# Loading the per-layer-embedding inputs later and storing their product from the ScalarE queue

## The chip, the cores and the metric

The kernel runs on one core of one Trainium2 chip. Five engines work side by side and meet at semaphores: TensorE (PE, its weight loads as PEld), VectorE (DVE), ScalarE (ACT), GpSimd (POOL) and SyncE (SP). The metric is the device time of one launch in microseconds. Transfers are issued from the instruction streams of SP, ACT and POOL and are carried out by 16 DMA engines that all of them share.

## The reference

Two transformer blocks over 512 tokens of width 1024, all in float32. The first has an mLSTM and differential attention mixer and then a mixture of experts; the second has pooling and window attention, a feed-forward layer and, at its very end, a gate over a product of per-layer inputs (`p_2`, 256 wide). The parts that matter here:

```python
def hierarchical_moe(h, ...):                      # first block, 32 experts, top 2 of one group
    g_sel = argmax(h @ w_group + b_group);  top_vals, top_idx = top_k(expert logits of the group, 2)
    ... sort the 1024 (token, expert) pairs by expert ...
    hid = silu(xb @ w_gate[e]) * (xb @ w_up[e]);  y = hid @ w_down[e]
    ...
def second_block(x, p, ..., w_ple, w_ple_gate, b_ple_gate):
    ...
    gate = sigmoid(h @ w_ple_gate + b_ple_gate)
    h = h + gate * (p @ w_ple)                     # p: 512 x 256, w_ple: 256 x 1024
```

`p @ w_ple` depends on nothing but inputs, so it can be computed at any time before the last line.

## The kernel before

The program is a hand-ordered instruction list for each engine. Work meets through counting semaphores; the eight PSUM banks are shared by "turns": `open_turn` waits until the bank's last reader has left it, `fill_turn` marks it full, `filled` waits for that, and `leave` and `left` mark and await that it is empty again. Which instruction stands where is only what is written in each engine's function.

The change lies in the passage from the mixer to the experts, about 335 to 395 us. What happens there:

- The last output projection pieces (`out_piece`), the residual, the second norm (`HN`), and its transposes (`turn_h`) give `HT`; `route(t)` multiplies it by the router weights. The normed rows are also stored to `h_rows` by ACT (`store_rows`), from where the experts' tokens are gathered.
- DVE turns the logits into one-hot choices (to `oh_ready`), PE counts ranks ("rank"), DVE makes positions (to `slots_hot`), PE multiplies them out ("slots"), DVE writes the indices, and POOL gathers the first block of token rows (L1140).
- PE transposes those rows (`turn_rows(0)`, L676), ACT copies them rounded into `XTS` (`rows_hi(0)`, L1423), DVE subtracts to get the rest (`rows_lo(0)`, L1945), and only then can the first expert product run (L687). Weights are split the same way: ACT writes a rounded copy `HI` in seven parts (`weights_hi`, L1419), DVE the remainder (`weights_lo`, L1940).
- The two small inputs of the last line are used here as well: `PIN` (p, 0.5 MB) and `PLEW` (w_ple, 1 MB) are loaded by two DMAs on the ACT queue (L1377, L1378), PE transposes PIN (four turns "pt"), ACT copies the transposes to `PET` (L1398), PE makes the product in eight pieces (`extra(n)`, L644), ACT copies each out of PSUM into one of three buffers (`extra_out(n)`, L1407), and SP stores it to `ple_rows` in HBM (L1016). Just before the end of the program it is read back.

The `extra` pieces stand on PE between the routing steps as filler: four before "rank", two before "slots", two behind. ACT interleaves its eight `extra_out` with the seven weight parts of expert 0. SP loads the experts' weights, three loads of 2 MB for each expert; the first load of the expert loop waits for `gate_raw_used`, which PE signals when the first product of the first expert block is done. 32 expert blocks follow one another in a loop.

Of the kernel before, what the change touches and what calls it, by code (L numbers as in the profile page):

```python
# [23 lines left out]
ACT = mybir.ActivationFunctionType  # L24
AX = mybir.AxisListType.X

P = 128
T = 512
D = 1024
TT = T // P  # L30
# [67 lines left out]
def build(nc, A, out):  # L98
    ctx = ExitStack()

    def sb(name, shape, dt=F32):
        return ctx.enter_context(nc.sbuf_tensor(name, shape, dt))

    def sem(name):
        return ctx.enter_context(nc.semaphore(name))

    with ctx:
# [4 lines left out]
        HT = sb("HT", [P, DT, T])  # L112
# [35 lines left out]
        def m(a, *shape):  # L148
            v = M[:, a:a + int(np.prod(shape))]
            if len(shape) == 2:  # L150
                v = v.rearrange("p (a b) -> p a b", a=shape[0])
            if len(shape) == 3:
                v = v.rearrange("p (a b c) -> p a b c", a=shape[0], b=shape[1])
            return v
# [36 lines left out]
        P2, DM = m(9936, TT), m(9940, TT)  # L191
# [28 lines left out]
        H5S = [as_r(f"h5s{k}", M_AT + a, DT, T) for k, a in enumerate((0, 8192))]  # L220
        GT = m(4096, 2, 512)
        OUT2 = m(12288, 2, TT, 512)
        PLEW, PIN, PET, PLE3 = m(12928, 2, D), m(1024, TT, 2 * P), m(16896, 2, T), m(2560, 3, 512)

        ps = ctx.enter_context(nc.psum_tensor("ps", [P, 8, 512], F32))
        h_rows = nc.dram_tensor("h_rows", [T, D], F32, kind="Internal").ap()
        ple_rows = nc.dram_tensor("ple_rows", [T, D], F32, kind="Internal").ap()
# [35 lines left out]
        r_dve = sem("r_dve")  # L263
        r_act = sem("r_act")
# [53 lines left out]
        ple_in = sem("ple_in")  # L318
        ple_out = [sem(f"ple_out{k}") for k in range(3)]
# [9 lines left out]
        def open_turn(pe, key, bank):  # L329
            turn[key] = (bank, turns_of[bank])  # L330
            if turns_of[bank]:
                pe.wait_ge(empty[bank], turns_of[bank])
            turns_of[bank] += 1
            return ps[:, bank, :]

        def fill_turn(ins, key):
            ins.then_inc(full[turn[key][0]], 1)

        def filled(eng, key):
            eng.wait_ge(full[turn[key][0]], turn[key][1] + 1)  # L340
            return ps[:, turn[key][0], :]

        def leave(ins, key):
            ins.then_inc(empty[turn[key][0]], 1)

        def left(eng, key):
            eng.wait_ge(empty[turn[key][0]], turn[key][1] + 1)
# [70 lines left out]
        def _(pe):  # L418
            def transposes(key, bank, src, n, width=P, idn=None):

                o = open_turn(pe, key, bank)
                idn = ident[:, :] if idn is None else idn
                for c in range(n):
                    ins = pe.transpose(o[:, c * width:(c + 1) * width], src[:, c * P:(c + 1) * P], idn)  # L424
                fill_turn(ins, key)
# [182 lines left out]
            def turn_h(t):  # L608
                for c in range(2):
                    pe.wait_ge(hn_ready, t + 1 + (c if t == TT - 1 else 0))  # L610
                    transposes(("h2", t, c), 2 + (2 * t + c) % 4, HN[:, t, c * 512:(c + 1) * 512], 4)

            def route(t):
                left(pe, ("h2", t, 0))
                left(pe, ("h2", t, 1))
                for k in range(DT):
                    ins = pe.matmul(ps[:, 7, t * E:(t + 1) * E], HT[:, k, t * P:(t + 1) * P], WR[:, k, :],
                                    start=(k == 0), stop=(k == DT - 1))
                return ins
# [11 lines left out]
            turn_h(2)  # L631
            out_piece(1, 3, 0, DT, 1)
            route(2)
            pe.wait_ge(ple_in, 32)
            for t in range(TT):
                transposes(("pt", t), t, PIN[:, t, :], 2)
            turn_h(3)
            fill_turn(route(3), "route")

            def extra(n):  # L640
                c, t = divmod(n, TT)
                o = open_turn(pe, ("pl", n), n % 4)
                for k in range(2):
                    ins = pe.matmul(o, PET[:, k, t * P:(t + 1) * P], PLEW[:, k, c * 512:(c + 1) * 512],  # L644
                                    start=(k == 0), stop=(k == 1))
                fill_turn(ins, ("pl", n))

            for t in range(TT):
                left(pe, ("pt", t))
            for n in range(4):  # L650
                extra(n)

            pe.wait_ge(oh_ready, 1)
# [3 lines left out]
                    ins = pe.matmul(o[:, t * NE:(t + 1) * NE], UPPER if j == t else ONESB,  # L657
                                    OHS[:, j, :], start=(j == 0), stop=(j == min(t, TT - 1)))
            fill_turn(ins, "rank")
            for n in range(4, 6):  # L660
                extra(n)

            pe.wait_ge(slots_hot, 1)
# [1 line left out]
            for j in range(2 * TT):  # L665
                ins = pe.matmul(o[0:BLK, 0:BLOCKS_HELD], POS1H[:, j, :], BLKV[:, j, :], start=(j == 0), stop=(j == 2 * TT - 1))
            fill_turn(ins, "slots")
            for n in range(6, 8):
                extra(n)


# [184 lines left out]
            for j, u in enumerate(FF_UNITS):  # L856
                n = int(u[-1])
# [47 lines left out]
            for c in range(2):  # L905
# [4 lines left out]
                for t in range(TT):  # L910
                    n = c * TT + t
# [16 lines left out]
        def _(sp):  # L928
# [80 lines left out]
            for s, u in last_use.items():  # L1009
                used_up(sp, u)  # L1010
                dst, src = first_loads[s]
                sp.dma_start(dst, src).then_inc(slot_in[s], 16)
            for n in range(2 * TT):
                c, t = divmod(n, TT)
                left(sp, ("pl", n))
                sp.dma_start(ple_rows[t * P:(t + 1) * P, c * 512:(c + 1) * 512], PLE3[:, n % 3, :]).then_inc(ple_out[n % 3], 16)  # L1016
            sp.wait_ge(tab_ready, 1)

            def freed(e, k):
# [24 lines left out]
            for n in range(2 * TT):  # L1044
                c, t = divmod(n, TT)
# [159 lines left out]
        def _(act):  # L1205
# [119 lines left out]
            def final_out(i, kind):  # L1325
                dst, gain = (MIXA, R_AN) if kind == "d" else (HT, R_MN)
                key = ("F", i, kind)
                q = filled(act, key).rearrange("p (h t) -> p h t", h=HEADS)
                leave(act.activation(dst[:, 0:HEADS, i * P:(i + 1) * P], q, ACT.Copy, scale=prm[:, gain:gain + 1]), key)
# [44 lines left out]
                        act.wait_ge(x_kept, t + 1)  # L1374
                        square_x(t)
            final_out(TT - 1, "m")
            act.dma_start(PIN, A["p_2"][0, 0].rearrange("(t p) c -> p t c", p=P)).then_inc(ple_in, 16)  # L1377
            act.dma_start(PLEW, A["w_ple_2"][0].rearrange("(k p) c -> p k c", p=P)).then_inc(ple_in, 16)  # L1378

            def store_rows(u):  # L1380
                act.wait_ge(hn_ready, u + 1 if u < TT - 1 else TT + 1)
                act.dma_start(h_rows[u * P:(u + 1) * P, :], HN[:, u, :]).then_inc(h_out, 16)
# [7 lines left out]
            for c in range(2):  # L1390
                left(act, ("o", c, TT - 1))
                acc = (7, 82)[c]
                act.activation(JUNK3[:, c * 512:(c + 1) * 512], X[:, TT - 1, c * 512:(c + 1) * 512], ACT.Square,
                               accum_out=st[:, acc:acc + 1]).then_inc(sumsq, 1)
                if c == 0:
                    store_rows(2)
            for t in range(TT):
                leave(act.activation(PET[:, :, t * P:(t + 1) * P],  # L1398
                                     filled(act, ("pt", t))[:, 0:2 * P].rearrange("p (k t) -> p k t", k=2), ACT.Copy), ("pt", t))
            leave(act.activation(HT[:, 4:8, (TT - 1) * P:T],  # L1400
                                 filled(act, ("h2", TT - 1, 1)).rearrange("p (k t) -> p k t", k=4), ACT.Copy), ("h2", TT - 1, 1))
            store_rows(3)

            def extra_out(n):
                if n >= 3:
                    act.wait_ge(ple_out[n % 3], 16 * (n // 3))
                leave(act.activation(PLE3[:, n % 3, :], filled(act, ("pl", n)), ACT.Copy), ("pl", n))  # L1407

            act.wait_ge(r_dve, 1)
            act.activation(EXPG, D4, ACT.Exp).then_inc(r_act, 1)  # L1410


            def weights_hi(e, part, odd):

                u, a, b = PARTS[part]
                s, c = expert_slots(odd)[u], slice(a, b)
                if a == 0:
                    act.wait_ge(slot_in[s], raw_loads(e, odd, s))
                act.activation(HI[u][:, c], ring[:, s, c], ACT.Copy).then_inc(w_hi, 1)  # L1419
# [38 lines left out]
            for part in range(7):  # L1458
                if part == 5:
                    filled(act, "slots")  # L1460
                    act.wait_ge(wts_ready, 1)
                weights_hi(0, part, 0)
                extra_out(part)
                if part == 2:
                    act.wait_ge(r_dve, 2)
                    act.activation(P2, DM, ACT.Exp).then_inc(r_act, 1)
            extra_out(7)
            act.wait_ge(tab_ready, 1)
            rows_hi(0)
            act.preload_act_table(ACT.Silu)  # L1470
# [671 lines left out]
```

## Time and profile before

| | us |
|---|---|
| median of 3 runs | 1514.16 (1513.98 to 1516.74) |
| the profiled execution | 1516.74 |
| its span in the trace | 1515.0 |
| PE busy | 1430.0 (94%) |
| DVE busy | 930.9 (61%) |
| ACT busy | 752.2 (50%) |

The profiled execution is the slowest of the three. Times in a trace count from the start of its span. "Released by" or "<-" names what ended a wait. A time inside the passage is read from the timeline of one engine: start, duration, line, operation, and how long the engine had idled before. float32 matmuls appear as two passes, so that one `extra` piece (two matmuls in the program) is four passes in the trace.

### The profile page before, as it was taken

What the parts mean: (1) busy time and instruction counts of PE and PEld (TensorE: products, weight loads), DVE (VectorE), ACT (ScalarE), POOL (GpSimd) and SP (SyncE); (2) the same over time, 40 slices, a digit from 0 to 9 for tenths busy, and PEclk for the clock granted to TensorE, in tenths of its full rate; (3) what the DMA queues carried; (4) which work ended last, traced back from release to release, by engine and by line L of the source; (5) the groups of instructions that cost most, each with busy time, mean ns of one, the idle gap of its engine ahead of it and who ended that gap; (6) DMA issues with size and microseconds to landing.
All of it is one profiled execution on the core that took longest, in us unless ns stands there. A gap on an engine that the chain in (4) does not pass through costs nothing.

```text
span 1515.0 us, 19584 instructions
## 1 busy us (share of the span) xinstructions
PE 1430.0 (94%) x6529; PEld 1047.6 (69%) x6530; DVE 930.9 (61%) x1129; ACT 752.2 (50%) x930; POOL 200.6 (13%) x234
## 2 busy tenths in 40 slices
PE   6899999999899999999999977988989999999998
PEld 6787667555677777777777754544468888888886
DVE  6845453354899999998989954272544413442275
ACT  4334334123699999998989840242124310333031
POOL 1011001000222222222212210041100000000010
PEclk8999999999999999999999997998989999999999
DMA  6131104315699999999999978300003321333231
GB/s 224 56 111 57 56 29 170 154 30 213 259 404 407 412 410 416 409 417 406 404 411 413 394 229 262 111 1 29 0 1 112 111 96 71 111 111 129 80 111 56
DMA packets 67892, 298.56 MB, mean 197 GB/s; under 512 B 18110, under 2 KB 20220, under 8 KB 55548
## 3 DMA queue, kind: packets, MB, share of 16 engines
q1 hardware_dynamic: 55036, 273.76, 46.6%
q10 hardware_dynamic: 7440, 15.63, 2.9%
q0 software_dynamic: 5360, 8.40, 1.7%
q8 instruction: 37, 0.61, 0.2%
q14 instruction: 19, 0.16, 0.0%
HBM read 292.00 MB, written 14.94 MB: 203 GB/s over the span
## 4 chain that ended last, share of the span: by engine, by line
PE 73%; DMA 6%; DVE 5%; issue 2%; ACT 2%; POOL 0%; ACTq 0%; DVEq 0%; SPq 0%; POOLq 0%
PE ps L687 12%; PE ps L869 12%; PE ps L887 11%; PE ps L725 6%; DMA ring<-in_w_gate 5%; PE ps L543 4%; PE ps L846 4%; PE ps L718 4%; PE ps L922 3%; PE ps L696 3%; PE ps L473 2%; PE ps L747 2%; PE ps L424 2%; PE ps L771 1%; PE ps L676 1%
## 5 line engine op out<-in xcount | busy, mean ns | idle before, releaser
L1940 DVE TENSOR_TENSOR ring_r<-ring,hi 128x2048 fp32r<-128x2048 f32 (+1 forms) x224 | 431.2, 1982 | 19.1 <-ACT hi L1419 17.1
L1419 ACT ACTIVATE hi<-ring 128x2048 fp32r<-128x2048 f32 (+1 forms) x224 | 363.0, 1662 | 13.3 <-DMA ring<-in_w_gate 8.3
L887 PE MATMUL ps<-ring_r,ats 128*128 128x512 f32 x768 | 174.7, 389 | 0.0
L887 PEld LDWEIGHTS ps<-ring_r,ats 128*128 128x128 f32 x768 | 144.1, 188 | 29.9
L1605 DVE TENSOR_TENSOR ring_r<-ring,ring_r 128x4096 fp32r<-128x4096 f32 x18 | 79.7, 4425 | 131.5 <-ACT ring_r L1225 131.5
L1225 ACT ACTIVATE ring_r<-ring 128x4096 fp32r<-128x4096 f32 x18 | 65.2, 3624 | 150.7 <-PE ps L887 122.0
L1088 POOL TENSOR_TENSOR rsv<-msv,half 128x1 f32<-128x1 f32 (+2 forms) x32 | 39.1, 1222 | 751.3 <-DVE msv L1565 731.4
L687 PE MATMUL ps<-ring_r,XTS 128*128 128x512 f32 x512 | 128.5, 393 | 3.9 <-DVE XTS L1945 2.1
L687 PE MATMUL ps<-hi,XTS 128*128 128x512 f32 x512 | 126.4, 389 | 0.0
L869 PE MATMUL ps<-ring_r,ring_r 128*128 128x512 f32 x512 | 123.3, 394 | 1.8 <-DVE hi L2056 1.8
L473 PE MATMUL ps<-ring_r,ring_r 128*128 128x512 f32 x448 | 117.2, 411 | 7.6 <-DVE M L1636 4.5
L725 PE MATMUL ps<-hi,HIDS 128*64 128x512 f32 x512 | 123.6, 394 | 0.0
L687 PEld LDWEIGHTS ps<-ring_r,XTS 128*128 128x128 f32 x512 | 96.9, 190 | 27.1 <-issue 4.9
L869 PEld LDWEIGHTS ps<-ring_r,ring_r 128*128 128x128 f32 x512 | 97.5, 191 | 22.6 <-issue 2.2
L687 PEld LDWEIGHTS ps<-hi,XTS 128*128 128x128 f32 x512 | 96.1, 188 | 20.0
L725 PEld LDWEIGHTS ps<-hi,HIDS 128*64 128x64 f32 x512 | 69.2, 135 | 50.0 <-issue 1.6
L473 PEld LDWEIGHTS ps<-ring_r,ring_r 128*128 128x128 f32 x448 | 85.4, 196 | 25.4 <-DVE M L1636 4.9
L718 PE MATMUL ps<-ring_r,HIDS 128*64 128x512 f32 x256 | 67.4, 407 | 6.2 <-ACT HIDS L1443 4.1
L696 PEld LDWEIGHTS ps<-M 128*128 128x128 f32 x512 | 64.5, 191 | 7.5 <-issue 3.6
L696 PE MATMUL ps<-M 128*128 128x64 f32 x512 | 64.8, 272 | 3.1 <-ACT M L1428 3.1
L1146 POOL DMA_INDIRECT results<-M,idx x33 | 49.1, 1488 | 128.8 <-ACT M L1451 128.4
L869 PE MATMUL ps<-hi,ring_r 128*128 128x512 f32 x256 | 63.2, 389 | 0.0
(307 smaller groups left out, 1851.7 us busy)
## 6 DMA issues: line engine op xcount, KB each, us to landing
ring<-in_w_up SPq DMA_DIRECT2D x32, 2048.0 KB, 18.4
ring<-in_w_gate SPq DMA_DIRECT2D x32, 2048.0 KB
ring<-in_w_down SPq DMA_DIRECT2D x32, 2048.0 KB, 16.9
ring<-in_w_ff SPq DMA_DIRECT2D x16, 2048.0 KB, 8.4
ring<-in_w_in SPq DMA_DIRECT2D x8, 2048.0 KB, 8.5
ring<-in_w_out SPq DMA_DIRECT2D x2, 2048.0 KB, 8.6
M<-results ACTq DMA_DIRECT2D x8, 512.0 KB, 7.5
ring<-in_w_ple_gate SPq DMA_DIRECT2D x2, 2048.0 KB, 7.8
```

The lines of the kernel that those rows point to most:

```text
L473: ins = pe.matmul(o, a, b, start=(i == 0 and k == 0), stop=(i == 2 and k == DT - 1))
L543: ins = pe.matmul(ps[:, bank, :], a, w[:, k, :], start=(k == 0), stop=(k == DT - 1))
L687: ins = pe.matmul(ps[:, u, :], XTS[:, k, :, :].rearrange("p s b -> p (s b)"), w[:, k, :], start=(part == 1 and k == 0), stop=(part == 0 an ...
L696: ins = pe.matmul(ps[:, bank, f * BLK:(f + 1) * BLK], GUS[:, u, f * P:(f + 1) * P], SUM2[:, 0:BLK], start=True, stop=True)
L718: ins = pe.matmul(ps[0:BLK, 4 + c, :], HIDS[:, 0, f, :], w_rest[:, f, c * 512:(c + 1) * 512], start=(f == 0), stop=False)
L725: ins = pe.matmul(ps[0:BLK, 4 + c, :], HIDS[:, a, f, :], w_top[:, f, c * 512:(c + 1) * 512], start=False, stop=(a == 1 and f == FT - 1))
L869: ins = pe.matmul(o, w[a][:, k, f * P:(f + 1) * P], HTS[b][:, k, :], start=(i == 0 and k == 0), stop=(i == 2 and k == DT - 1))
L887: ins = pe.matmul(ps[:, 2 * t + c, :], ATS[a][:, 4 * (n % 4) + k, t * P:(t + 1) * P], w[b][:, k, c * 512:(c + 1) * 512], start=(n % 4 == 0 ...
L1225: act.activation(split_hi[j % 2][:, :], ring[:, s, :], ACT.Copy).then_inc(s_hi, 1)
L1419: act.activation(HI[u][:, c], ring[:, s, c], ACT.Copy).then_inc(w_hi, 1)
L1605: vec.tensor_tensor(ring_r[s][:, :], ring[:, s, :], split_hi[j % 2][:, :].bitcast(F32), ALU.subtract).then_inc(s_lo, 1)
L1940: vec.tensor_tensor(ring_r[s][:, c], ring[:, s, c], HI[u][:, c].bitcast(F32), ALU.subtract).then_inc(w_lo, 1)
```

## The change

On SP the eight stores to `ple_rows` are gone; ACT issues each of them, right behind the copy that fills the buffer, once that copy has ended. On ACT the loads of PLEW and PIN move from before the square of row tile 2 to behind the square of the last half tile, and PLEW now goes first; the four PET copies move behind the last `HT` copy and the last `store_rows`; two `extra_out` and both small exponentials (EXPG, P2) now stand ahead of the first weight part, the other six `extra_out` behind parts 0, 1, 2, 4, 5 and 6. On PE the transposes of PIN move behind the last `route`, and use banks 4 and 5 in turn instead of banks 0 to 3; the pieces are dealt 2, 3, 3 instead of 4, 2, 2. PIN lies 512 elements further in `M`.

```diff
-        ... PIN ... m(1024, TT, 2 * P)
+        ... PIN ... m(1536, TT, 2 * P)
@@ tensor
             route(2)
-            pe.wait_ge(ple_in, 32)
-            for t in range(TT):
-                transposes(("pt", t), t, PIN[:, t, :], 2)
             turn_h(3)
             fill_turn(route(3), "route")
...
+            pe.wait_ge(ple_in, 32)
+            for t in range(TT):
+                transposes(("pt", t), 4 + t % 2, PIN[:, t, :], 2)
             for t in range(TT):
                 left(pe, ("pt", t))
-            for n in range(4):
+            for n in range(2):
                 extra(n)
... rank ...
-            for n in range(4, 6):
+            for n in range(2, 5):
                 extra(n)
... slots ...
-            for n in range(6, 8):
+            for n in range(5, 8):
                 extra(n)
@@ sync
-            for n in range(2 * TT):
-                c, t = divmod(n, TT)
-                left(sp, ("pl", n))
-                sp.dma_start(ple_rows[...], PLE3[:, n % 3, :]).then_inc(ple_out[n % 3], 16)
             sp.wait_ge(tab_ready, 1)
@@ scalar
             final_out(TT - 1, "m")
-            act.dma_start(PIN, ...).then_inc(ple_in, 16)
-            act.dma_start(PLEW, ...).then_inc(ple_in, 16)
...
-            for t in range(TT):
-                leave(act.activation(PET[...], filled(act, ("pt", t)) ...), ("pt", t))
+            act.dma_start(PLEW, ...).then_inc(ple_in, 16)
+            act.dma_start(PIN, ...).then_inc(ple_in, 16)
             leave(act.activation(HT[:, 4:8, (TT - 1) * P:T], ...), ("h2", TT - 1, 1))
             store_rows(3)
+            for t in range(TT):
+                leave(act.activation(PET[...], filled(act, ("pt", t)) ...), ("pt", t))
 
             def extra_out(n):
+                c, t = divmod(n, TT)
                 if n >= 3:
                     act.wait_ge(ple_out[n % 3], 16 * (n // 3))
                 leave(act.activation(PLE3[:, n % 3, :], filled(act, ("pl", n)), ACT.Copy), ("pl", n))
-
+                left(act, ("pl", n))
+                act.dma_start(ple_rows[...], PLE3[:, n % 3, :]).then_inc(ple_out[n % 3], 16)
+
+            extra_out(0)
+            extra_out(1)
             act.wait_ge(r_dve, 1)
             act.activation(EXPG, D4, ACT.Exp).then_inc(r_act, 1)
+            act.wait_ge(r_dve, 2)
+            act.activation(P2, DM, ACT.Exp).then_inc(r_act, 1)
...
                 weights_hi(0, part, 0)
-                extra_out(part)
-                if part == 2:
-                    act.wait_ge(r_dve, 2)
-                    act.activation(P2, DM, ACT.Exp).then_inc(r_act, 1)
-            extra_out(7)
+                if part in (0, 1, 2, 4, 5, 6):
+                    extra_out((2, 3, 4, None, 5, 6, 7)[part])
```

On PE, between the router products (L617) and the transposes of the first gathered rows (L676), a piece of the difference of the two orders; L424 are transposes, L644 (L641 in the changed file) the `extra` pieces, L657 "rank", L666 "slots":

```order
 L617 MATMUL ps<-M,HT 128x36 x8
-L424 MATMUL ps<-ident,M 128x128 x16
+L424 MATMUL ps<-ident,M 128x128 x8
 L617 MATMUL ps<-M,HT 128x36 x8
-L644 MATMUL ps<-M 128x512 x8
+L424 MATMUL ps<-ident,M 128x128 x8
+L641 MATMUL ps<-M 128x512 x4
 L657 MATMUL ps<-M 128x32 x14
-L644 MATMUL ps<-M 128x512 x4
+L641 MATMUL ps<-M 128x512 x6
 L666 MATMUL ps<-M 64x58 x8
-L644 MATMUL ps<-M 128x512 x4
+L641 MATMUL ps<-M 128x512 x6
```

The eight transposes of PIN have moved behind the last router product, two pieces (four matmuls) stand ahead of "rank" instead of four, and three instead of two on each side of "slots".

On ACT, before, from the loads of PIN and PLEW (L1377, L1378) to the first small exponential (L1410); L1334 and L1393 are squares, L1382 stores of `h_rows`, L1398 the PET copies, L1400 the last `HT` copy:

```order
L1377 DMA M<-in_p 128x4x256
L1378 DMA M<-in_w_ple 128x2x1024
L1334 ACTIVATE M,st<-X 128x1024
L1382 DMA h_rows<-M 128x1024 x2
L1393 ACTIVATE M,st<-X 128x512
L1382 DMA h_rows<-M 128x1024
L1393 ACTIVATE M,st<-X 128x512
L1398 ACTIVATE M<-ps 128x2x128 x4
L1400 ACTIVATE HT<-ps 128x4x128
L1382 DMA h_rows<-M 128x1024
L1410 ACTIVATE M<-M 128x16
```

The same place afterwards, from the square of row tile 2 (L1330 now) to the first copy of a piece (L1403), with the squares at L1386, the stores of `h_rows` at L1375 and the PET copies at L1396:

```order
L1330 ACTIVATE M,st<-X 128x1024
L1375 DMA h_rows<-M 128x1024 x2
L1386 ACTIVATE M,st<-X 128x512
L1375 DMA h_rows<-M 128x1024
L1386 ACTIVATE M,st<-X 128x512
L1390 DMA M<-in_w_ple 128x2x1024
L1391 DMA M<-in_p 128x4x256
L1392 ACTIVATE HT<-ps 128x4x128
L1375 DMA h_rows<-M 128x1024
L1396 ACTIVATE M<-ps 128x2x128 x4
L1403 ACTIVATE M<-ps 128x512
```

Both loads now stand behind the last square, and the last store of `h_rows` stands behind them in the same queue.

On ACT again, the weight parts of expert 0 (copies into `hi`), before, with the copies of the pieces at L1407 and the exponential P2 at L1466:

```order
L1410 ACTIVATE M<-M 128x16
L1419 ACTIVATE hi_57<-ring 128x2048
L1407 ACTIVATE M<-ps 128x512
L1419 ACTIVATE hi_57<-ring 128x1024
L1407 ACTIVATE M<-ps 128x512
```

And afterwards, with the copies at L1403 and their stores at L1405:

```order
L1403 ACTIVATE M<-ps 128x512
L1405 DMA ple_rows<-M 128x512
L1403 ACTIVATE M<-ps 128x512
L1405 DMA ple_rows<-M 128x512
L1410 ACTIVATE M<-M 128x16
L1412 ACTIVATE M<-M 128x4
L1421 ACTIVATE hi_57<-ring 128x2048
L1403 ACTIVATE M<-ps 128x512
L1405 DMA ple_rows<-M 128x512
L1421 ACTIVATE hi_57<-ring 128x1024
```

The first weight part now stands behind two copies and their stores, and each later copy has a DMA issue between it and the next weight part.

## Rows read from the trace of the kernel before

**Rows 1.** The page, chain of waits by engine, whole span.
```profile
PE 73%; DMA 6%; DVE 5%; issue 2%; ACT 2%; POOL 0%; ACTq 0%; DVEq 0%; SPq 0%; POOLq 0%
```

**Rows 2.** Chain of waits in time, expert loop: start us, us, what.
```profile
674.11 19.57 DMA ring<-in_w_gate
```

**Rows 3.** The same view, 325 to 425 us.
```profile
364.38 8.64 PE ps L644 x16
...
378.91 1.15 PE ps L666 x16
...
383.06 4.56 DVE ring_r L1940 x3
...
387.64 0.70 DVE XTS L1945
...
389.05 8.94 PE ps L687 x32
```

**Rows 4.** Timeline of ACT: start us, us, engine, line, operation, idle before.
```profile
335.77 0.39 ACTq L1377 DMA_DIRECT2D M<-in_p  x1
336.19 0.53 ACTq L1378 DMA_DIRECT2D M<-in_w_ple  x1
336.84 1.06 ACT L1334 ACTIVATE M<-X 128x1024 f32<-128x1024 f32 x1 [0.39 <-issue]
...
358.12 0.63 ACT L1393 ACTIVATE M<-X 128x512 f32<-128x512 f32 x1 [12.16 <-DVE X L1777]
...
367.14 1.91 ACT L1419 ACTIVATE hi<-ring 128x2048 fp32r<-128x2048 f32 x1 [1.68 <-DMA h_rows<-M]
368.96 0.58 ACT L1407 ACTIVATE M<-ps 128x512 f32<-128x512 f32 x1
369.44 1.05 ACT L1419 ACTIVATE hi<-ring 128x1024 fp32r<-128x1024 f32 x1
370.38 0.59 ACT L1407 ACTIVATE M<-ps 128x512 f32<-128x512 f32 x1
...
372.28 0.21 ACT L1466 ACTIVATE M<-M 128x4 f32<-128x4 f32 x1
...
387.01 0.60 ACT L1423 ACTIVATE XTS<-ps 128x512 fp32r<-128x512 f32 x1 [1.76 <-PE ps L676]
```

**Rows 5.** Timeline of PE.
```profile
358.83 1.07 PE L424 MATMUL ps<-ident,M 128*128 128x128 f32 x8
...
379.98 3.70 PE L644 MATMUL ps<-M 128*128 128x512 f32 x8
386.23 0.68 PE L676 MATMUL ps<-ident,M 64*128 64x64 f32 x8 [2.55 <-DMA M<-h_rows,idx]
```

**Rows 6.** Timeline of PE's weight loads, two consecutive passes of the pieces.
```profile
365.49 0.34 PEld L644 LDWEIGHTS ps<-M 128*128 128x128 f32 x1 [0.51 <-issue]
366.35 0.34 PEld L644 LDWEIGHTS ps<-M 128*128 128x128 f32 x1 [0.52 <-issue]
```

**Rows 7.** Timeline of SP.
```profile
357.32 0.33 SPq L1012 DMA_DIRECT2D ring<-in_w_up  x1
369.56 16.03 SPq L1016 DMA_DIRECT2D ple_rows<-M  x8
392.73 0.36 SPq L1028 DMA_DIRECT2D ring<-in_w_gate  x1
```

**Rows 8.** DMA issues, 325 to 400 us: count, KB each, us from issue to landing.
```profile
M<-in_w_ple ACTq DMA_DIRECT2D x1, 1024.0 KB, 7.4
M<-in_p ACTq DMA_DIRECT2D x1, 512.0 KB, 3.5
```

**Rows 9.** The same view, 355 to 392 us.
```profile
ring<-in_w_up SPq DMA_DIRECT2D x1, 2048.0 KB, 8.5
ple_rows<-M SPq DMA_DIRECT2D x8, 256.0 KB, 2.0
h_rows<-M ACTq DMA_DIRECT2D x1, 512.0 KB, 5.4
```

**Rows 10.** Windows: busy of each engine, then PE clock, DMA share, GB/s.
```profile
360.00:365.00 5.00, 3.65 (x26) 3.19 (x27) 2.05 (x5) 1.09 (x3) 0.00 (x0) 0.98 0.98 409
365.00:366.00 1.00, 1.00 (x2) 0.34 (x1) 0.83 (x6) 0.22 (x1) 0.00 (x0) 0.50 0.26 102
```

More of the change, by code:

```diff
@@ L222, in build @@
         OUT2 = m(12288, 2, TT, 512)
-        PLEW, PIN, PET, PLE3 = m(12928, 2, D), m(1024, TT, 2 * P), m(16896, 2, T), m(2560, 3, 512)
+        PLEW, PIN, PET, PLE3 = m(12928, 2, D), m(1536, TT, 2 * P), m(16896, 2, T), m(2560, 3, 512)
         ps = ctx.enter_context(nc.psum_tensor("ps", [P, 8, 512], F32))
@@ L1012, in _ @@
                 sp.dma_start(dst, src).then_inc(slot_in[s], 16)
-            for n in range(2 * TT):
-                c, t = divmod(n, TT)
-                left(sp, ("pl", n))
-                sp.dma_start(ple_rows[t * P:(t + 1) * P, c * 512:(c + 1) * 512], PLE3[:, n % 3, :]).then_inc(ple_out[n % 3], 16)
             sp.wait_ge(tab_ready, 1)
@@ L1376, in _ @@
             final_out(TT - 1, "m")
-            act.dma_start(PIN, A["p_2"][0, 0].rearrange("(t p) c -> p t c", p=P)).then_inc(ple_in, 16)
-            act.dma_start(PLEW, A["w_ple_2"][0].rearrange("(k p) c -> p k c", p=P)).then_inc(ple_in, 16)
             def store_rows(u):
@@ L1396, in _ @@
                     store_rows(2)
+            act.dma_start(PLEW, A["w_ple_2"][0].rearrange("(k p) c -> p k c", p=P)).then_inc(ple_in, 16)
+            act.dma_start(PIN, A["p_2"][0, 0].rearrange("(t p) c -> p t c", p=P)).then_inc(ple_in, 16)
+            leave(act.activation(HT[:, 4:8, (TT - 1) * P:T],
+                                 filled(act, ("h2", TT - 1, 1)).rearrange("p (k t) -> p k t", k=4), ACT.Copy), ("h2", TT - 1, 1))
+            store_rows(3)
             for t in range(TT):
@@ L1399, in _ @@
                                      filled(act, ("pt", t))[:, 0:2 * P].rearrange("p (k t) -> p k t", k=2), ACT.Copy), ("pt", t))
-            leave(act.activation(HT[:, 4:8, (TT - 1) * P:T],
-                                 filled(act, ("h2", TT - 1, 1)).rearrange("p (k t) -> p k t", k=4), ACT.Copy), ("h2", TT - 1, 1))
-            store_rows(3)
             def extra_out(n):
+                c, t = divmod(n, TT)
                 if n >= 3:
@@ L1407, in extra_out @@
                 leave(act.activation(PLE3[:, n % 3, :], filled(act, ("pl", n)), ACT.Copy), ("pl", n))
+                left(act, ("pl", n))
+                act.dma_start(ple_rows[t * P:(t + 1) * P, c * 512:(c + 1) * 512], PLE3[:, n % 3, :]).then_inc(ple_out[n % 3], 16)
+            extra_out(0)
+            extra_out(1)
             act.wait_ge(r_dve, 1)
             act.activation(EXPG, D4, ACT.Exp).then_inc(r_act, 1)
+            act.wait_ge(r_dve, 2)
+            act.activation(P2, DM, ACT.Exp).then_inc(r_act, 1)
             def weights_hi(e, part, odd):
```

## The prediction

> **What bounds the kernel now.** I read the page's chain of waits first: PE holds 73% of it and DMA 6% [rows 1], so the kernel is mostly one long PE string with a few places where PE is released by something else. The chain in time shows two kinds of such places. In the expert loop a 2 MB weight load decides now and then (19.57 us at 674.11) [rows 2]; that load is one of a series that SP starts only when PE has finished the first product of the first expert block, at 392.73 [rows 7]. And in the passage that the change touches, the chain leaves PE and comes back to it at 389.05, when the first expert product starts [rows 3]. Everything behind, PE's 32 blocks and SP's stream of loads, hangs on that moment. So the question is when that first product (L687) can start.
>
> Before, two things released it nearly together. The routing path: pieces on PE from 364.38 to 373.02, then "rank", DVE, "slots" at 378.91, the index, the gather, the transposes of the gathered rows at 386.23 [rows 3, 5], the ACT copy at 387.01 [rows 4], DVE's remainder at 387.64, PE at 389.05 [rows 3]. And DVE's three gate parts, which ended at 387.62 (383.06 + 4.56) [rows 3]. ACT was not a bound: it had idled 1.76 us before 387.01 [rows 4]. The reader is to see that ACT has nearly no reserve there, since `rows_hi(0)` stands behind all of its weight parts and piece copies.
>
> **When the inputs arrive.** PLEW's load now goes out just behind the square that starts at 358.12 [rows 4], so at about 358.2, and PIN's behind it. Before, they were issued at 335.77 and 336.19 [rows 4] and landed 3.5 and 7.4 us later [rows 8], by 343.6, 15 us before PE's transposes of PIN at 358.83 [rows 5]. Now nothing hides them: route(3) ends on PE at 364.38, where the pieces started [rows 3]. And they meet SP's 2 MB load of the `up` weights, issued at 357.32 [rows 7], which took 8.5 us [rows 9], in a stretch in which the DMA engines were already at a share of 0.98 and moved 409 GB/s [rows 10]. PIN's 0.52 MB would take 1.3 us at that rate and took 3.5, so 2.2 us of a transfer are start and landing. With half of 409 GB/s for the ACT queue, 1.57 MB take 7.7 us: 358.2 + 2.2 + 7.7 = 368.1. Bounds: as before without company, 336.19 + 7.4 - 335.77 = 7.8 us, 366.0; all of the load, both inputs and the h_rows store first (4.2 MB at 409 GB/s = 10.2 us), 370.6. I take the middle one, because h_rows' 0.5 MB, issued at 361.70 while the weight load was under way, landed in 5.4 us [rows 9] beside it and not after a full turn.
>
> That agrees with the Trainium skill, "DMA: Bandwidth & Descriptors", section on queues, rings and completion order: each DMA engine goes round the queues that have work, a packet at a time. By it the ACT queue gets about its half, as in the 368.1; if one queue were served to its end first, the sum would start from 370.6 instead, and the result would be 2.5 us later.
>
> **PE up to "rank".** Eight transposes took 1.07 us [rows 5] at full clock. But PE has now nothing from 364.4 to 368.1, and already before the granted clock was 0.50 (the 1.2 GHz level) at 365 to 366 [rows 10], where the passes stood 0.86 us apart (365.49, 366.35) [rows 6] against 0.44 at full clock (3.70 us for eight, less 0.59 for the last to drain, over seven) [rows 5]. So I take the transposes at half clock, 2.1 us, plus 0.3 for the last PET copy (half the width of a 0.59 us copy [rows 4]; an estimate): pieces start at 370.5. Two pieces are eight passes: 3.5 us at full clock, 6.9 at half. Before, four passes ran at the low clock; with the transposes counted I take two here: 2 x 0.86 + 6 x 0.44 = 4.3, so piece 1 ends at 374.8 (370.9 at best: 366.0, full clock; 379.9 at worst: 370.6, half clock). "Rank" then starts 1.8 us later than before (373.02), though it has two pieces fewer ahead of it. Behind it, three pieces of four passes (5.3 us) fit beside DVE's work, which ran from 373.4 to "slots" at 378.91. Rows would be gathered 1.8 us late, about 388.0.
>
> **ACT to rows_hi(0).** This is the term that I expect to decide. In order: the copy of piece 1 (0.6), then its store. A DMA issue holds the ACT stream: the square at 336.84 waited 0.39 us although the engine was free, until both issues were over (336.19 + 0.53 = 336.72, and 0.12 more) [rows 4]. A store of this size took 0.33 to issue (the nearest row is SP's 0.33 [rows 7]), and it has to wait for its copy's end first, so that nothing overlaps: 0.60 + 0.33 + 0.12 = 1.05 us for each copy with its store, against 0.48 before (368.96 to 369.44) [rows 4]. Piece 1 is out at 375.85; the two small exponentials add about 0.3 (0.21 the one) [rows 4]: the first weight part starts at 376.15, where it started at 367.14 before [rows 4]. From there: five parts of 2048 at 1.82 (367.14 to 368.96) = 9.1; two of 1024 at 0.94 (369.44 to 370.38) = 1.9; six copies with stores at 1.05 = 6.3. Sum 17.3, end 393.4. Neither "slots" nor a free buffer adds a wait (a store lands in 2.0 us [rows 9]). rows_hi(0) thus starts at 393.4 instead of 387.01, **6.4 us later**, and 5 us after its rows are there.
>
> **The rest.** Behind rows_hi(0) stand DVE's rows_lo(0) and the last four weight remainders of expert 0, in order, so DVE cannot work ahead; the first product moves to 395.4, SP's first load of the loop from 392.73 to 399.1. SP's eight stores gone: nothing, SP next waits for that load's release anyway [rows 7]. The last store of h_rows behind the inputs in ACT's queue lands at 370 instead of 367.1: nothing, since ACT and POOL come to it after 376. Eight transposes less ahead of turn_h(3): nothing, they filled PE's wait for the norm. PIN's address: nothing. The stores' wait before the loop (393.4 + 2.0) ends inside the wait for the first product. If the low clock came earlier because PE lacks those transposes, route(3) would end a microsecond or so later, still before 368.1.
>
> Sum: +6.4 us. On the profiled execution 1516.74 gives 1523.1; that one was the slowest of three, and from the median 1514.16 I forecast **1520.5 us**. Its own range: with the best arrival and full clock 370.9 in place of 374.8, +2.5; with the worst 379.9, +11.5: 1516.7 to 1525.7.
>
> **Rivals.**
> A, not slower: the stores cost ACT nothing and the inputs arrive early, so that the routing path decides and gains by the shorter queue ahead of "rank". Piece 1 ends at 370.9, "rank" starts 2.1 us earlier; ACT: 370.9 + 0.5 + 0.3 + 17.3 - 6 x 0.57 = 385.6, that is 1.4 us before 387.01. Time 1512.8. For it: two pieces ahead of "rank" instead of four, which was the wait of DVE there. Against: it needs landing by 366.0 beside a saturated DMA, a PE clock that stays up over an idle stretch, and free issues; the break-even is piece 1 out of ACT by about 370, and the row at 336.84 speaks against the last.
> B, no change: only the issues are free (they overlap the copies). 7 x 0.57 = 4.0 less: +2.4, 1516.6. Against it the 0.39 us row and the wait for the copy.
> C, hidden anyway: the delay is taken up in the expert loop, where loads decide at times [rows 2]; 1514.2. Against: the loads start by the same event.
> D, much slower: inputs at 370.6 and the pieces all at half clock: +11.5, 1525.7. For it: PE idles nearly 4 us or more before them.
>
> **How the numbers follow.** My forecast 0.65, A 0.06, B 0.10, C 0.08, D 0.11. A measurement of this kernel tells some 0.2% (3 us) from no change. B and C lie within it, of my forecast only its low end (0.02 of the 0.65), and of A half (its gain could be twice what I work out, if the gather's way is shorter too); so slower 0.63 + 0.11 = 0.74, same 0.10 + 0.08 + 0.02 + 0.03 = 0.23, faster 0.03. The range leaves out A, C in the main and the top of D: 1515.0 to 1524.5.
>
> **What would show it.** In the trace after: the loads of PLEW and PIN issued near 358.2 and landing near 368; PE idle from 364.4 until then; "rank" near 374.8; the first weight part on ACT near 376.2 and gaps of 0.5 us behind each piece copy; rows_hi(0) near 393.4 with no idle ahead of it; the first L687 near 395.4, and a constant distance behind that. It is wrong if ACT idles before rows_hi(0), if "rank" comes before 373, or if the loop is shorter than before.

## The result and the profile after

The changed kernel takes 1524.95 us (median of 6 runs, 1524.71 to 1525.88) against 1514.12 us before (6 runs, 1510.77 to 1516.74): 1.0069 times as long, 95% interval 1.0058 to 1.0081 (the ratio is taken over more runs than the medians, 23 of the changed kernel). That is 10.8 us more, where 6.4 were forecast. The direction was right, and so was the engine that decides (ACT); the size was not, and the time lies just outside the range (1515.0 to 1524.5).

The page's chain of waits of the changed kernel, beside [rows 1]:

```profile
PE 75%; DMA 4%; DVE 4%; ACT 2%; issue 2%; ACTq 0%; POOL 0%; DVEq 0%; SPq 0%; POOLq 0%
```

ACT has grown by nothing that a share would show; the passage has to be read in time. Everything below is counted from t0, the start of the last residual on VectorE, since up to there PE does the same work in both. (The two profiled executions differ by 2.4 us already at 333 us, ahead of anything that the change touches. That is why their spans, 1515.0 and 1523.2 us, lie 8.2 us apart and not 10.5.) First the kernel before, then the changed one (start, duration, engine, line, operation, idle before):

```profile
357.40 0.69 DVE L1777 TENSOR_TENSOR X<-M,ps 128x512 f32<-128x512 f32 x1 [7.10 <-PE ps L543]
```
```profile
355.03 0.69 DVE L1776 TENSOR_TENSOR X<-M,ps 128x512 f32<-128x512 f32 x1 [7.40 <-PE ps L543]
```

The chain of waits in time, changed kernel, from t0 to the first expert product (compare [rows 3]):

```profile
356.19 11.52 DMA M<-in_p
...
370.71 6.51 PE ps L641 x8
...
378.56 1.80 ACT hi L1421
...
396.08 0.70 DVE XTS L1944
...
397.17 8.98 PE ps L687 x32
```

Before, the chain went from route(3) into the pieces, "rank", DVE, the gather. Now it waits 11.5 us for the load of PIN, goes through the transposes and the pieces, and then stays on ACT, weight part and copy in turn, up to rows_hi(0). The first product starts at t0+42.1 (397.17 - 355.03) against t0+31.65 (389.05 - 357.40): 10.5 us later. Behind it nothing is made good. The first transposes behind the expert loop, before and after:

```profile
913.23 1.97 PE L424 MATMUL ps<-ident,X 128*128 128x128 f32 x8 [12.49 <-DVE X L1978]
```
```profile
921.41 1.97 PE L424 MATMUL ps<-ident,X 128*128 128x128 f32 x8 [12.43 <-DVE X L1977]
```

They stand 524.2 us behind the first product in both.

ACT in the changed kernel (compare [rows 4]): the issues of the two loads, pieces 0 and 1, and what follows them (L1403 copies a piece, L1405 stores it, L1421 is a weight part, L1425 rows_hi(0)):

```profile
355.76 0.40 ACTq L1390 DMA_DIRECT2D M<-in_w_ple  x1
356.19 1.05 ACTq L1391 DMA_DIRECT2D M<-in_p  x1
...
374.50 0.60 ACT L1403 ACTIVATE M<-ps 128x512 f32<-128x512 f32 x1 [4.04 <-PE ps L641]
...
377.25 0.60 ACT L1403 ACTIVATE M<-ps 128x512 f32<-128x512 f32 x1 [2.15 <-PE ps L641]
...
378.46 1.89 ACT L1421 ACTIVATE hi<-ring 128x2048 fp32r<-128x2048 f32 x1
380.26 0.58 ACT L1403 ACTIVATE M<-ps 128x512 f32<-128x512 f32 x1
380.87 0.33 ACTq L1405 DMA_DIRECT2D ple_rows<-M  x1
381.24 1.06 ACT L1421 ACTIVATE hi<-ring 128x1024 fp32r<-128x1024 f32 x1 [0.40 <-ACT M L1403]
...
395.45 0.60 ACT L1425 ACTIVATE XTS<-ps 128x512 fp32r<-128x512 f32 x1 [0.46 <-ACT M L1403]
```

Each store costs as expected: from the copy at 380.26 to the next weight part at 381.24 are 0.98 us, where 0.48 were before [rows 4]. ACT never waits for the gathered rows.

PE in the changed kernel (compare [rows 5]):

```profile
360.07 3.60 PE L617 MATMUL ps<-M,HT 128*128 128x36 f32 x16 [0.78 <-ACT HT L1392]
367.76 2.27 PE L424 MATMUL ps<-ident,M 128*128 128x128 f32 x8 [4.09 <-DMA M<-in_p]
370.71 6.50 PE L641 MATMUL ps<-M 128*128 128x512 f32 x8 [0.68 <-ACT M L1396]
377.04 0.51 PE L657 MATMUL ps<-M 128*128 128x32 bf16 x14
...
389.74 0.68 PE L676 MATMUL ps<-ident,M 64*128 64x64 f32 x8 [0.17 <-issue]
```

The gathered rows are turned at 390.4 and ACT fetches them at 395.45: 5 us of reserve on the routing path. The surprise is the clock. Windows of the changed kernel (busy of PE, PEld, DVE, ACT, POOL, then PE clock, DMA share, GB/s):

```profile
355.00:358.00 3.00, 1.63 (x15) 1.51 (x14) 2.20 (x4) 0.72 (x2) 0.58 (x2) 1.00 0.70 213
358.00:360.00 2.00, 1.09 (x8) 0.86 (x8) 1.23 (x3) 0.60 (x1) 0.00 (x0) 0.84 0.98 414
360.00:363.00 3.00, 2.93 (x14) 2.96 (x15) 0.00 (x0) 0.00 (x0) 0.00 (x0) 0.50 0.95 399
363.00:366.00 3.00, 0.67 (x4) 0.53 (x3) 1.95 (x9) 0.00 (x0) 0.00 (x0) 0.50 0.94 282
...
376.00:377.00 1.00, 1.00 (x3) 0.40 (x2) 0.00 (x0) 0.00 (x0) 0.00 (x0) 0.80 0.66 248
```

It falls to the 1.2 GHz level before route(3) (360.07); PE had been busy 1.63 us of the three before 358 and 1.09 of the two behind, since the PIN transposes that filled this wait are gone. (e9 and e7 below bear this out.) It comes back only at the end of piece 1. In the kernel before, the level was still 0.98 over 360 to 365 and 0.50 only behind it [rows 10], and route(3) took 1.95 us:

```profile
362.44 1.95 PE L617 MATMUL ps<-M,HT 128*128 128x36 f32 x16 [0.78 <-ACT HT L1400]
```

The transfers of the changed kernel between 355 and 392 (count, KB each, us from issue to landing), and SP's issue of the weight load:

```profile
ring<-in_w_up SPq DMA_DIRECT2D x1, 2048.0 KB, 8.3
...
M<-in_w_ple ACTq DMA_DIRECT2D x1, 1024.0 KB, 10.0
M<-in_p ACTq DMA_DIRECT2D x1, 512.0 KB, 11.5
```
```profile
354.95 0.33 SPq L1012 DMA_DIRECT2D ring<-in_w_up  x1
```

The weight load took no longer than before (8.5) [rows 9]; the inputs took the whole delay, 7.4 and 3.5 us [rows 8] having become 10.0 and 11.5.

### The profile page after: what moved, and what is told of

It reads as the page before. It is cut to its first block, busy times and chain, and to the rows that moved or that the text cites. A ratio compares the mean times of both kernels' runs of the same rounds, so it can differ in the third digit from the quotient of the medians.

```text
span 1523.2 us, 19584 instructions
## 1 busy us (share of the span) xinstructions
PE 1434.7 (94%) x6529; PEld 1050.1 (69%) x6530; DVE 930.9 (61%) x1129; ACT 752.6 (49%) x930; POOL 198.3 (13%) x234
## 4 chain that ended last, share of the span: by engine, by line
PE 75%; DMA 4%; DVE 4%; ACT 2%; issue 2%; ACTq 0%; POOL 0%; DVEq 0%; SPq 0%; POOLq 0%
PE ps L687 14%; PE ps L869 12%; PE ps L887 11%; PE ps L725 7%; PE ps L718 4%; PE ps L543 4%; PE ps L846 4%; PE ps L696 3%; PE ps L922 3%; DMA ring<-in_w_gate 3%; PE ps L473 2%; PE ps L747 2%; PE ps L424 2%; PE ps L771 1%; PE ps L676 1%
## 5 line engine op out<-in xcount | busy, mean ns | idle before, releaser
L1939 DVE TENSOR_TENSOR ring_r<-ring,hi 128x2048 fp32r<-128x2048 f32 (+1 forms) x224 | 431.3, 1982 | 18.3 <-ACT hi L1421 16.3
L1421 ACT ACTIVATE hi<-ring 128x2048 fp32r<-128x2048 f32 (+1 forms) x224 | 362.8, 1662 | 8.8 <-DMA ring<-in_w_gate 6.7
L687 PEld LDWEIGHTS ps<-ring_r,XTS 128*128 128x128 f32 x512 | 97.1, 190 | 32.2 <-issue 10.0
L473 PEld LDWEIGHTS ps<-ring_r,ring_r 128*128 128x128 f32 x448 | 87.5, 201 | 26.1 <-DVE M L1635 4.9
## 6 DMA issues: line engine op xcount, KB each, us to landing
ring<-in_w_down SPq DMA_DIRECT2D x32, 2048.0 KB, 16.4
```

Source lines behind the costliest of these rows:

```text
L473: ins = pe.matmul(o, a, b, start=(i == 0 and k == 0), stop=(i == 2 and k == DT - 1))
L687: ins = pe.matmul(ps[:, u, :], XTS[:, k, :, :].rearrange("p s b -> p (s b)"), w[:, k, :], start=(part == 1 and k == 0), stop=(part == 0 an ...
L1939: vec.tensor_tensor(ring_r[s][:, c], ring[:, s, c], HI[u][:, c].bitcast(F32), ALU.subtract).then_inc(w_lo, 1)
```

## The experiments

Ten kernels ran. The ratio is that of the run against the kernel before on the same chip; t0-times, in us, are from each kernel's trace. Diffs and lines are excerpts, and `...` stands for what is left out.

| kernel | piece 1 on ACT | rank | rows_hi(0) | first product | ratio to before (95%) |
|---|---|---|---|---|---|
| before | 13.0 | 15.5 | 29.6 | 31.65 | 1 |
| changed | 22.2 | 22.0 | 40.4 | 42.1 | 1.0069 (1.0058 to 1.0081) |
| e1 loads early | 18.3 | 18.1 | 36.5 | 38.2 | 1.0047 (1.0031 to 1.0064) |
| e2 stores on SP | 21.8 | 21.6 | 36.6 | 38.3 | 1.0056 (1.0035 to 1.0076) |
| e3 both | 18.3 | 18.1 | 33.0 | 34.8 | 1.0020 (1.0009 to 1.0032) |
| e6 weight load later | 16.6 | 16.4 | 34.8 | 36.5 | 1.0040 (1.0027 to 1.0053) |
| e7 PE kept busy | 18.7 | 18.5 | 36.9 | 38.7 | 1.0044 (1.0027 to 1.0061) |
| e8 weight parts first | 22.2 | 22.0 | 37.7 | 39.4 | 1.0058 (1.0041 to 1.0075) |
| e4 before, stores on ACT | 12.5 | 15.5 | 29.5 | 31.8 | 0.9997 (0.9985 to 1.0009) |
| e5 before, dealing 2, 3, 3 | 12.8 | 12.2 | 26.4 | 28.5 | 0.9978 (0.9967 to 0.9989) |
| e9 e5 and ACT's new order | 12.2 | 12.2 | 27.2 | 29.0 | 0.9978 (0.9962 to 0.9994) |
| e10 e5, PE kept busy | 12.2 | 12.2 | 26.1 | 28.2 | 0.9955 (0.9943 to 0.9968) |

**e1, the loads early.**

```diff
             final_out(TT - 1, "m")
+            act.dma_start(PIN, ...); act.dma_start(PLEW, ...)
...
-            act.dma_start(PLEW, ...); act.dma_start(PIN, ...)
```

PIN also has its old address again and is issued first, as in the kernel before.

> The changed kernel with the two input loads back at their old place on ScalarE (before the square of row tile 2); everything else as changed. I count from the start of the last residual on VectorE (t0): the first expert product starts at t0+31.7 us in the kernel before and t0+42.1 in the changed one. My theory (the late inputs delay the pieces, and the pieces delay ScalarE, whose string of weight parts, copies and stores takes 18.2 us from piece 1 to rows_hi(0)): PIN is there, so its transposes follow route(3) at about t0+8.6; with 3 us for them and 4.3 to 6.5 us for two pieces, piece 1 is out at t0+16 to t0+18 instead of t0+22.2, rows_hi(0) at t0+34 to t0+36, the first product at t0+36 to t0+38: 4.3 to 6.3 us slower than before. Rival (the loads are the whole cause): as fast as before, t0+32.

PE in e1:

```profile
360.98 3.60 PE L617 MATMUL ps<-M,HT 128*128 128x36 f32 x16 [0.78 <-ACT HT L1392]
364.38 2.26 PE L424 MATMUL ps<-ident,M 128*128 128x128 f32 x8
367.31 6.75 PE L641 MATMUL ps<-M 128*128 128x512 f32 x8 [0.68 <-ACT M L1396]
```

The transposes follow route(3) at once, and all three still run at the low clock. The first product comes at 38.2, just above what was expected (36 to 38), and so do piece 1 (18.3) and rows_hi(0) (36.5); the kernel is about 7 us slower than before. The late arrival is worth 4.0 us of the 10.5 (42.14 - 38.17), and not the whole.

**e2, the stores on SP.** The loop of stores stands in SP's list again, and `extra_out` has no wait and no DMA.

> The changed kernel with the eight stores back on SyncE; the inputs stay late. Theory: the stores on ScalarE cost seven times 0.57 us between piece 1 and rows_hi(0) (18.2 us becomes about 14.2), ScalarE stays the last to be ready by about 1 us over the gathered rows (transposed at t0+35.4), so the first product starts at t0+38 and the kernel is 6 to 7 us slower than before. Rival (the issues are not what makes ScalarE late, or the gathered rows decide): t0+41 to t0+42, 10 us slower.

ACT in e2 at the same place as above, and the end of its string:

```profile
379.36 0.59 ACT L1407 ACTIVATE M<-ps 128x512 f32<-128x512 f32 x1
379.83 1.05 ACT L1423 ACTIVATE hi<-ring 128x1024 fp32r<-128x1024 f32 x1
...
391.64 0.61 ACT L1427 ACTIVATE XTS<-ps 128x512 fp32r<-128x512 f32 x1
```

0.47 us from copy to weight part; piece 1 to rows_hi(0) takes 14.8 us instead of 18.2. The first product at 38.3 as expected, 3.8 us earlier than in the changed kernel (that 0.4 of it is an earlier piece 1 belongs to the inputs). The measured time, 8.5 us over before (5.3 to 11.5), holds the 6.6 that the trace gives.

**e3, both undone.**

> Both undone: inputs loaded early, stores on SyncE; what stays of the change is the place of PIN's transposes behind route(3), two pieces and both exponentials ahead of the first weight part on ScalarE, and the dealing 2, 3, 3. Theory: the two costs add up, so the first product starts about 4 us earlier than with the loads early alone, at t0+32 to t0+34: 0 to 2 us slower than before. Rival (the new order itself is the cost): still over 4 us slower.

At 34.8 the two costs add up (42.1 - 4.0 - 3.8 = 34.3), but something is left: 3.1 us by the trace, 3.0 by the ratio, more than the 0 to 2 that I had expected. Either the new order on ACT or the place of PIN's transposes; e9 tells them apart.

**e6, the inputs alone on the DMA engines.**

```diff
                 used_up(sp, u)
+                if s == 4:
+                    sp.wait_ge(ple_in, 32)
```

> The changed kernel, but SyncE's load of the up weights of expert 0 (2 MB) waits until both inputs have landed, so the inputs have the DMA engines to themselves. Theory (sharing with that load is what made them land 12 us after the first issue): they land in about 8 us, the pieces start 4 us earlier, and the first product at t0+38: 6 to 7 us slower than before. Rival 1 (the time is PIN's own, its 1 KB rows and its 1.05 us issue): landing unchanged, t0+42. Rival 2 (the clock eats it: the pieces run low whenever TensorE has idled): landing 4 us earlier, pieces as slow as in the changed kernel, still t0+38.

DMA issues of e6 (count, KB each, us from issue to landing), and then its pieces on PE:

```profile
M<-in_w_ple ACTq DMA_DIRECT2D x1, 1024.0 KB, 5.1
M<-in_p ACTq DMA_DIRECT2D x1, 512.0 KB, 6.1
```
```profile
366.43 5.21 PE L641 MATMUL ps<-M 128*128 128x512 f32 x8 [0.68 <-ACT M L1398]
```

Against 10.0 and 11.5 us in the changed kernel: 5.4 us are the company of the weight load, more than the 4 I had expected, and more than the whole effect of the late loads on the first product (4.0). The pieces gain another 1.3 us, since the clock comes back earlier (0.73 in 369 to 370). Why it does is open: PE no longer idles ahead of PIN's transposes, but it doesn't in e1 and e3 either, and their pieces took 6.75 and 6.68 us. The first product is at 36.5, 5.6 us earlier than changed. The time (6 us over before, 4 to 8) fits the trace's 4.9.

**e7, PE kept busy.**

```diff
             route(2)
+            spare(2)      # 2 matmuls 128x128 by 128x512 into bank 6, read by nobody
             turn_h(3)
             fill_turn(route(3), "route")
+            spare(4)
```

> The changed kernel with matmuls added on TensorE whose product nobody reads: two ahead of the transposes of the last row tile and four behind route(3), where it idled. Theory (the low clock after the idle stretch costs 1.6 us in route(3), some 1 us in PIN's transposes and 2.8 us in the first two pieces): granted clock 1.0 through, piece 1 out 3.5 to 4 us earlier, the first product at t0+38 to t0+38.6, 6.5 to 7 us slower than before. Rival (the pieces are slow for another reason): t0+42.

PE in e7, route(3) and the two pieces:

```profile
360.77 1.95 PE L617 MATMUL ps<-M,HT 128*128 128x36 f32 x16 [0.78 <-ACT HT L1400]
...
370.76 3.67 PE L649 MATMUL ps<-M 128*128 128x512 f32 x8 [0.68 <-ACT M L1404]
```

1.95 for 3.60 and 3.67 for 6.50: the clock was worth 3.5 us of the changed kernel's way to piece 1, though the inputs landed as late as there (11.5 us). 38.7 and 6.7 us over before, as expected. That the clock would stay at 1.0 throughout was wrong: it was low under the four later spare matmuls (0.61 in 365 to 367), although PE had worked without a gap since 361. That cost nothing, since the inputs had not landed.

**e8, weight parts ahead of the pieces' copies.** Parts 0 to 2 stand behind the PET copies, parts 3 to 6 behind pieces 2 to 5, pieces 6 and 7 last.

> The changed kernel with ScalarE's order altered: the first three weight parts stand behind the PET copies and ahead of piece 0, and the fourth to seventh are dealt among the later pieces. Theory (ScalarE's string is late because it idles 4.0 + 2.2 us for pieces 0 and 1 while weight parts that it could do stand behind them): rows_hi(0) 2.8 us earlier, the first product at t0+39.3, 7.5 to 8 us slower than before. Rival (the arrival of the inputs alone sets the time): no change from the changed kernel, t0+42.

ACT in e8:

```profile
372.07 3.79 ACT L1413 ACTIVATE hi<-ring 128x2048 fp32r<-128x2048 f32 x3
376.22 0.60 ACT L1403 ACTIVATE M<-ps 128x512 f32<-128x512 f32 x1 [0.36 <-PE ps L641]
```

The idle 4.0 us ahead of piece 0 is filled, and rows_hi(0) comes 2.7 us earlier (2.8 expected) though piece 1 is out at 22.2 as in the changed kernel. So the arrival acts through the order of ACT's list, as the prediction had it. The time, 8.8 us over before (6.2 to 11.4), holds the trace's 7.8.

**e4, the kernel before with the stores on ACT.**

> The kernel before with one thing of the change: ScalarE issues the eight stores, each behind its copy (1.05 us for copy and store in place of 0.48). Theory (a cost on ScalarE counts only where ScalarE is the last to be ready): five of them fall before ScalarE waits for the slots product anyway (it had idled there 3.0 us), three behind it, 1.7 us, which its idle 1.76 us ahead of rows_hi(0) just takes up. rows_hi(0) at t0+29.6 as before, give or take 0.3; the kernel as fast as before. Rival (the issues cost wherever they stand): 3 to 4.5 us slower.

ACT in e4, the last store and rows_hi(0):

```profile
384.75 0.33 ACTq L1406 DMA_DIRECT2D ple_rows<-M  x1
385.29 0.60 ACT L1422 ACTIVATE XTS<-ps 128x512 fp32r<-128x512 f32 x1 [0.58 <-PE ps L676]
```

The same eight issues cost nothing here: ACT is done 0.2 us before PE has turned the rows. They cost 3.8 us in the changed kernel because ACT is the last to be ready there.

**e5, the kernel before with the dealing 2, 3, 3.**

> The kernel before with only the dealing of the pieces changed to 2, 3, 3 (PIN's transposes and loads, the stores and ScalarE's order stay as before). Theory: the rank product had waited on TensorE behind pieces 2 and 3; it now starts when the one-hot choices are ready, at about t0+12.2 instead of t0+15.5, the gathered rows come 3.2 us earlier, ScalarE and VectorE follow, and the first product starts at t0+28.4: 3 us faster than before (0.2%). Rival (the clock or ScalarE holds it): no change.

PE in e5:

```profile
362.91 5.38 PE L644 MATMUL ps<-M 128*128 128x512 f32 x8
368.33 0.52 PE L657 MATMUL ps<-M 128*128 128x32 bf16 x14
```

"Rank" at 12.2 instead of 15.5, the first product at 28.5, and 0.9978 of the time before: 3.3 us faster (1.7 to 5.0). This one part of the change is a gain; "rank" comes 3.2 us earlier, where rival A had put 2.1.

**e9, e5 with ACT's new order.**

> The kernel before with the dealing 2, 3, 3 and with ScalarE's order as in the change (pieces 0 and 1 and both exponentials ahead of the first weight part, the others behind parts 0, 1, 2, 4, 5, 6); loads, stores and PIN's transposes as before. Theory (the order on ScalarE is harmless when the pieces come early): piece 1 is out at t0+12.3, ScalarE's string without stores takes 14.1 us from there, so it is ready for rows_hi(0) at about t0+26.5, as the gathered rows are; first product at t0+28.5 to t0+29.5, 2 to 3 us faster than before. Rival (the order alone costs what was left in the run with both undone, 3.2 us): t0+32 or later.

First product at 29.0, 0.9978: the new order on ACT costs 0.4 us in the trace and nothing that can be measured. e9 differs from e3 only in where PE transposes PIN (with the banks used, and with the four PET copies standing ahead of ACT's last HT copy instead of behind it). So the 5.8 us between them (34.8 - 29.0) are the move of those eight transposes behind route(3): 1.65 us of low clock in route(3), some 3 us of transposes and copies now in the way (2.9 from their start to the pieces), and pieces 1.1 us slower.

**e10, e5 with PE kept busy ahead of the first product.**

```diff
             turn_rows(0)
+            pe.wait_ge(empty[1], turns_of[1])
+            for _ in range(2):
+                pe.matmul(ps[:, 1, :], ident[:, :], X[:, 0, 0:512], start=True, stop=True)
```

> The kernel before with the dealing 2, 3, 3 and two matmuls on TensorE, whose product nobody reads, behind the transposes of the first gathered rows. Theory (the first product runs at the 1.2 GHz level because TensorE has idled before it, and SyncE's loads of the loop hang on its end): the clock stays up, the first product takes 1.8 instead of 3.5 us and the loads start 1.7 us earlier; 4 to 5 us faster than before. Rival (VectorE's remainders of the up weights, not the clock, set the second product and so the rest): as fast as the dealing alone, 3 us faster than before.

The first two products and SP's first load of the loop, in e5 and then in e10:

```profile
384.62 3.75 PE L687 MATMUL ps<-ring_r,XTS 128*128 128x512 f32 x8 [2.22 <-DVE XTS L1945]
388.17 3.23 PE L687 MATMUL ps<-hi,XTS 128*128 128x512 f32 x8
...
388.56 0.36 SPq L1028 DMA_DIRECT2D ring<-in_w_gate  x1
```
```profile
382.36 2.09 PE L687 MATMUL ps<-ring_r,XTS 128*128 128x512 f32 x8 [0.23 <-issue]
384.29 1.98 PE L687 MATMUL ps<-hi,XTS 128*128 128x512 f32 x8
...
384.63 0.36 SPq L1031 DMA_DIRECT2D ring<-in_w_gate  x1
```

The first load goes out at t0+30.4 instead of t0+32.5, and the kernel takes 0.9955 of the time before, 6.8 us less (4.8 to 8.6), somewhat more than the 4 to 5 expected. Against e5 it is 3.5 us, twice the 1.7 expected of the first product: the second product gains too (3.23 to 1.98 us), so that the third starts 3.0 us earlier (t0+32.2 against t0+35.2). With 1508.06 us in the median it beats both kernels, and e5 too, if narrowly (their intervals just touch).

## Why the prediction was right in kind and wrong in size

**What bounds the kernel** was read rightly: the first product is the moment on which the rest hangs. It moved by 10.5 us, the kernel by 10.8, and the loop behind it kept its 524.2 us. Rival C is out.

**ACT as the last to be ready** held. Predicted from piece 1's end to rows_hi(0): 393.4 - 374.8 = 18.6 us; measured 395.45 - 377.25 = 18.2. e2 and e4 show the stores' part of it (3.4 us in the string, and nothing where ACT has reserve), e8 the part of the order. Rival B is out: the issues are not free. Rival A named a gain that exists (e5) but is buried.

**The failed step is "PE up to rank", piece 1's end:** predicted 374.8 - 357.4 = t0+17.4, measured t0+22.2. Three terms of it:
- The inputs' landing: predicted t0+10.7 (368.1), measured t0+12.7, 2.0 us more. I had given the ACT queue half of 409 GB/s while the weight load ran. It got less, as the DMA queues from 355 us to the weight load's landing at 363.25 (354.95 + 8.3) show (packets, MB, share of 16 engines; q1 is SP's queue, which had just this load, and q10 ACT's):

```profile
q1 hardware_dynamic: 144, 2.10, 67.1%
q10 hardware_dynamic: 164, 0.67, 20.0%
```

  So the inputs, with the store of h_rows behind them, had a quarter of the traffic up to there. And that store moved along with the inputs: when PIN landed, 4.1 of the 4.2 MB of all four transfers had moved (326 GB/s over 355 to 367.7). The inputs thus came when nearly everything had come, close to the upper bound that I had set aside (370.6, t0+13.2). By an estimate the weight load's 2.1 MB are 5.1 us at 409 GB/s; e6, where it waits, was 5.4 us shorter. The row by which I chose the middle value could not tell the two apart: h_rows landed at 367.1, behind the weight load beside it (357.32 + 8.5 = 365.8).
- Transposes and PET copies: 2.4 predicted, 2.95 measured.
- The two pieces: 4.3 predicted with two of eight passes at the low clock, 6.5 measured, since nearly all ran low. I had taken the four low passes of the kernel before as a budget of low time that the transposes would already use up. e7 shows that the whole difference to 3.7 us is the clock. This is the largest error, 2.2 us.

Together 4.8 us; less 0.4 on ACT and 0.3 behind it they make 4.1, which is what lay between 6.4 and 10.5. Rival D, with all pieces at half clock and the inputs later still, had piece 1's end at t0+22.5 and gave 11.5; it was the nearest, in the mechanism too, and had a chance of 0.11.

**A term costed at nothing was wrong:** "eight transposes less ahead of turn_h(3): nothing". Their time was hidden, but the clock was not: route(3) took 3.60 instead of 1.95 us. I had noted that case and shown that it doesn't matter while the inputs arrive later, which is right for the changed kernel; in e1 and e3, where the inputs are there, it is part of what is left.

By the experiments the 10.5 us come out as a sum: the dealing and ACT's order -2.7 (31.65 to 29.0, e9), PIN's transposes behind route(3) +5.8 (to 34.8, e3), the stores on ACT +3.4 (to 38.2, e1), the late loads +4.0 (to 42.1). Of the largest term the prediction had only the 2.4 us of transposes and copies. The split hangs a little on the order: with the stores undone first (e2), they come to 3.8 and the loads to 3.5.

On the Trainium skill's rule that a DMA engine goes round the queues that have work, a packet at a time ("DMA: Bandwidth & Descriptors", queues, rings and completion order): the trace agrees, 144 packets of SP's queue moved beside 164 of ACT's. But SP's were 14.6 KB in the mean and ACT's 4.1 KB. The rule says nothing of equal bytes; reading it so was my error, and by halves the inputs would have landed 2 us earlier. That the size of the packets set the shares is argued from these counts; no run varied it.

What stays open: what brings the clock back when it does (e6's pieces against those of e1 and e3), and whether its early fall or PE's idle 4.1 us keeps the pieces of the changed kernel low, since e7 filled both. The kernel's time also deviates by 1 to 3 us from what the first product gives in e6 and e10. In single profiles the way from the first product to the transposes behind the loop was 529.2 us in e6 and 521.4 in e10, against 524.2; the clock under the first two products explains about 1 us of either, the rest is open, and the intervals are about 4 us wide.

## What to carry to other kernels

A load that is moved to "just in time" has to be priced in company with what else is in flight and with the clock that its wait leaves behind, not by its own landing time. Beside another load in flight, don't price it by half of the rate: look at the packets and bytes of each queue in a trace. Filler on TensorE does two jobs here, its own work and keeping the clock up; when it is moved out of a short wait, look at the matmuls on both sides of that wait. And a cost added to an engine counts only from the point where that engine is the last to be ready: the same eight DMA issues were free in one order and cost 3.4 us in another.

## What the runs showed of the hardware

- In the changed kernel TensorE's granted clock was 0.50 from before route(3) to the end of piece 1 (0.80 in 376 to 377), through 4 us of idling and two broken stretches of work. At that level the same sixteen passes of route(3) took 3.60 instead of 1.95 us, eight passes of the pieces 6.50 instead of 3.67.
- Two loads of 1.57 MB took 5.1 and 6.1 us from issue to landing without a weight load beside them and 10.0 and 11.5 beside a 2 MB load on another queue. While that load ran, its queue moved 144 packets of 14.6 KB in the mean, the inputs' queue 164 of 4.1 KB.
- An issue on ScalarE can take longer when transfers are in flight: PIN's, second in line, took 0.49 us without the weight load (e6) and 1.05, 0.87, 0.94 and 0.97 beside it (changed kernel, e2, e7, e8); it covered no work here, as ACT was waiting anyway.
